# Eight instead of six of 22 pairs of k tiles of each w_down half by seven block products

## The reference

```python
h = rmsnorm(x, g_ffn_pre[l])
ff = (jax.nn.silu(h @ w_gate[l]) * (h @ w_up[l])) @ w_down[l]
x = x + rmsnorm(ff, g_ffn_post[l])
```

## Time and profile before

| | us |
|---|---|
| median of 3 runs | 1199.53 |
| lowest, highest | 1198.66, 1199.59 |
| profiled execution, its own time | 1201.28 |
| its span in the trace | 1199.6 |
| PE busy | 1184.5 |
| DVE busy | 986.0 |
| ACT busy | 686.1 |
| POOL busy | 77.5 |

### The profile page before, as it was taken

One profiled execution on the slowest core, in us unless ns is written; L12 is line 12 of the kernel. 1 busy time (PEld: TensorE's weight loads), 2 busy tenths in 40 slices (PEclk: granted clock), 3 DMA queues, 4 the chain that ended last, 5 costly groups with the idle time before them and its releaser, 6 DMA issues.

```text
span 1199.6 us, 16437 instructions
## 1 busy us (share of the span) xinstructions
PE 1184.5 (99%) x5733; PEld 993.7 (83%) x5733; DVE 986.0 (82%) x1314; ACT 686.1 (57%) x924; POOL 77.5 (6%) x85
## 2 busy tenths in 40 slices
PE   8999999999999999999999999999999999999997
PEld 7888888888888888888888888888888888888885
DVE  6656777876786755879999999999999789879877
ACT  5654666474654744665556566665655555546543
POOL 1000100000000000001110110111010001000100
PEclk9999999999999999999999999999999999999999
DMA  8656867767785655566575667657565766655653
GB/s 313 207 158 158 226 174 157 181 141 183 184 188 173 224 186 195 173 235 195 193 239 185 202 207 228 202 182 247 187 198 200 246 210 211 210 176 196 213 188 140
DMA packets 124596, 237.23 MB, mean 198 GB/s; under 512 B 8312, under 2 KB 24960, under 8 KB 123392
## 3 DMA queue, kind: packets, MB, share of 16 engines
q1 hardware_dynamic: 122784, 231.05, 62.1%
q0 software_dynamic: 1760, 5.51, 1.7%
HBM read 229.97 MB, written 4.20 MB: 195 GB/s over the span
## 4 chain that ended last, share of the span: by engine, by line
PE 87%; DVE 5%; DMA 5%; ACT 1%; issue 1%; SPq 0%; DVEq 0%; ACTq 0%
PE bank L1787 85%; DMA raw<-in_w_in 4%; DVE w_lo L1132 2%; DMA resid<-in_x 1%; PE bank L2064 1%; ACT w_hi L711 1%; DVE w_lo L1618 0%; PE bank L1792 0%; PE bank L1981 0%; DVE more_lo L1618 0%; DVE raw L1635 0%; DVE v_sb L1259 0%; DVE gT L1346 0%; DVE h L1159 0%; DVE resid L1780 0%
## 5 line engine op out<-in xcount | busy, mean ns | idle before, releaser
L1132 DVE TENSOR_TENSOR w_lo<-raw,w_hi 128x1024 fp32r<-128x1024 f32 x172 | 209.2, 1223 | 121.6 <-ACT w_hi L711 121.1
L711 ACT ACTIVATE w_hi<-raw 128x1024 fp32r<-128x1024 f32 x172 | 180.5, 1057 | 164.5 <-PE bank L1787 142.4
L1787 PE MATMUL bank<-hT,w_hi 128*128 128x512 f32 x768 | 270.7, 396 | 1.4 <-DVE w_lo L1132 1.4
L1787 PE MATMUL bank<-w_hi,h2T 128*128 128x512 f32 x778 | 253.4, 391 | 0.0
L1787 PE MATMUL bank<-hT,w_lo 128*128 128x256 f32 x768 | 214.5, 279 | 0.0
L1787 PEld LDWEIGHTS bank<-hT,w_hi 128*128 128x128 f32 x768 | 143.9, 187 | 33.5 <-DVE w_lo L1132 2.0
L1787 PEld LDWEIGHTS bank<-w_hi,h2T 128*128 128x128 f32 x778 | 146.1, 188 | 30.1
L1615 DVE TENSOR_TENSOR w_lo<-raw,w_hi 128x1024 fp32r<-128x1024 f32 x110 | 133.5, 1230 | 19.4 <-ACT w_hi L1022 18.6
L1787 PE MATMUL bank<-w_lo,h2T 128*128 128x512 f32 x379 | 147.5, 389 | 0.0
L1787 PEld LDWEIGHTS bank<-hT,w_lo 128*128 128x128 f32 x768 | 145.0, 189 | 0.0
L1618 DVE TENSOR_TENSOR w_lo<-raw,w_hi 128x1024 fp32r<-128x1024 f32 x126 | 134.6, 1105 | 2.3 <-ACT w_hi L1036 1.7
(11 more groups left out here) (265 smaller groups left out, 1808.4 us busy)
## 6 DMA issues: line engine op xcount, KB each, us to landing
raw<-in_w_in SPq DMA_DIRECT2D x63, 1024.0 KB, 11.0
raw<-in_w_down SPq DMA_DIRECT2D x88, 512.0 KB, 5.0
raw<-in_w_up SPq DMA_DIRECT2D x80, 512.0 KB, 3.9
raw<-in_w_gate SPq DMA_DIRECT2D x80, 512.0 KB, 4.7
raw<-in_w_out SPq DMA_DIRECT2D x16, 1024.0 KB, 5.0
raw<-in_w_gate SPq DMA_DIRECT2D x4, 1024.0 KB, 5.2
raw<-in_w_up SPq DMA_DIRECT2D x4, 1024.0 KB, 6.4
raw<-raw POOLq DMA_DIRECT2D x9, 256.0 KB, 5.7
```

The lines of the kernel that those rows point to most:

```text
L711: act.activation(part_of(w_hi, rnd, s), src, ACT.Copy).then_inc(hi_done, 1)
L1132: dve.tensor_tensor(part_of(w_lo, rnd, s), raw_sub(rnd, s)[1], part_of(w_hi, rnd, s).bitcast(F32), ALU.subtract).then_inc(lo_done, 1)
L1787: return pe.matmul(out_, lhsT, rhs, start=start, stop=stop, skip_group_check=True)
```

## The change

Two plan strings differ. The first half (`DOWN`) had S units 3, 6, 9, 12, 15 and 18, and has 3, 5, 8, 10, 13, 15, 18 and 20. The second half (`LAST_HALF`) had 2, 5, 8, 11, 14 and 17, and has 3, 5, 7, 9, 11, 13, 15 and 17. All counts of pieces, loads, waits and sums follow from the strings. Each half has 60 pieces instead of 56. The last S unit of the first half is unit 20 instead of 18, so that one R unit stands behind it, where there were three.

```diff
 FULL = Plan("RRSSRSSR")
 FINAL = Plan("RRSSRRRR")
-DOWN = Plan("RRRSRRSRRSRRSRRSRRSRRR")
-LAST_HALF = Plan("RRSRRSRRSRRSRRSRRSRRRR")
+DOWN = Plan("RRRSRSRRSRSRRSRSRRSRSR")
+LAST_HALF = Plan("RRRSRSRSRSRSRSRSRSRRRR")
 LAST_HALF.pieces[-8:] = [(n, piece) for piece in range(2) for n in range(18, 22)]
 DOWN_PLANS = (DOWN, LAST_HALF)
```

## The result

The changed kernel takes 1202.98 us (median of 10 runs, 1202.03 to 1204.23) against 1199.56 for the kernel before (10 runs). The ratio is 1.0027, 95% interval 1.0019 to 1.0035: slower by 3.4 us, where 4.8 was forecast. The profiled execution took 1203.55 us.

The account below looks back on a forecast made before the run. PE was taken to bound the kernel while VectorE delivers. Second half: stalls 0.6 + 6.2 + 0.1 = 6.9 us less 1.36 of products, +5.5; first half -0.7; together +4.8 on 1199.53, so 1204.3 us, range 1201.9 to 1206.9.

Parts of the forecast that it names:

- The bound: w_down halves: PE bounds while VectorE delivers; afterwards VectorE bounds the second half's R S stretch; 58% for this forecast.
- The price of a pair: VectorE time per unit: S 8.06 us plus 1.11 for a GpSimd collision, R 2.28; R S 11.45 against PE's 10.21.
- Unit 5 of the second half: Its operands, ready 1.1 us early before the change, come late and stall PE by 0.6 us.
- T: The time at which PE starts the second half, 1075.67 before; VectorE's partial sums were to start at T - 4.5.
- The last period: Second half, unit 15 to 17: no GpSimd subtraction left, VectorE takes 10.34 us, 0.1 us of stall.
- The first half: 0.7 us of stall at unit 5, taken between 0.1 and 1.2, less 1.36 of products: -0.7 us.
- The gap at unit 3: First half's first S unit: PE's wait for operands stays at 0.72 us, as unit 3 is S before and after.
- collisions cost little: Rival for both halves: GpSimd collisions fall where VectorE waits, no stall, net -2.7 us, 1196.8 us; 6%.
- half of them land harmless: Rival: half the collisions are harmless or more lead is handed over; stalls 3 to 4.5 us, 1200.5 us; 9%.
- a second chain joins: Rival, second half: ScalarE's rounding also delays VectorE, 0.4 us in each of six periods, +2.4 us, 1206.7 us; 10%.
- The first half stalled less than forecast and not more: Rival: first half stalls 1.2 us at unit 5 and 0.5 at units 10 and 15, +1.5 us, 1205.8 us; 15%.
- the partial sums were done: Rival at the half boundary: VectorE over 1.9 us behind with the partial sums, so PE stops, +1 us more; 2%.

Follow-up runs that it names:

- experiment 3: Changed kernel with GpSimd subtracting only 8 of the 512 columns for each w_down S unit; 1196.61 us, ratio 0.9964 to the kernel before.
- experiment 6: Changed kernel with GpSimd's subtraction replaced by a ScalarE negation and an adding DMA; 1196.50 us, ratio 0.9967 to the kernel before.
- experiment 7: Changed kernel with GpSimd writing a constant to the same block instead of subtracting; 1196.72 us, ratio 0.9964 to the kernel before.
- experiment 4: Kernel before with seven S units in each half, 3 5 8 10 13 15 18 and 3 5 8 10 13 15 17; 1197.74 us, ratio 0.9980.
- experiment 2: Kernel before with only the second half changed to eight S units, six in the first as before; 1203.22 us, ratio 1.0028.
- experiment 10: Kernel before, old plans, with only the block sum moved from GpSimd to ScalarE and a DMA; 1198.94 us, ratio 0.9993.
- experiment 1: Kernel before with only the first half changed to eight S units, six in the second as before; 1198.26 us, ratio 0.9985.
- experiment 5: Kernel before with eight S units in the first half and seven in the second (3 6 8 11 13 15 17); 1197.46 us, ratio 0.9977.
- experiment 8: Changed kernel with GpSimd doing its subtraction twice for each w_down S unit; 1215.64 us, ratio 1.0125 to the kernel before.

## Why the prediction was right, point by point

- *The bound.* Right. The chain shows PE's unbroken run broken up in the second half and nowhere else, and there PE starts each S unit 0.06 us after L1749. That d_ops is the deadline that ends last, before w_lo, is what PE's timeline shows.
- *The price of a pair.* 8.06 + 2.28 = 10.34 us for R S without a collision: 10.35 in experiments 3, 6 and 7. The collision was priced 1.11 and is 0.97 here. It falls on the d_sum of L1725 and not on L1749. That this d_sum has only 128 columns is not the reason: in experiment 4 the one of L1722 lost the full 1.1 us (at 1145.71, below). L1725 begins 0.32 us behind L1722, where two d_sum without a pause are 0.20 apart; that it so comes 0.12 late to GpSimd's instruction would fit, but was not tested. So a period is 11.32 instead of 11.45. In five periods that is 0.7 of the 6.2 us. It is the largest term that was mis-sized.

```profile
1144.64 2.31 POOL L671 TENSOR_TENSOR raw<-raw 128x512 f32<-128x512 f32 x1 [8.01 <-DMA raw<-in_w_down]
1145.71 1.38 DVE L1722 TENSOR_TENSOR d_sum<-d_sum,d_whole 128x128 f32<-128x128 f32 x1
```

- *Unit 5 of the second half.* The operands were to come 0.6 us late; PE was held up by 0.3. VectorE began its partial sums at T - 4.6 instead of T - 4.5, and the two collisions on the way cost 0.97 each. The delay by the last S unit at 20 was real: experiment 2, without it, has unit 5 early by 1.1.
- *The last period* without a collision: 10.35, so 0.14 of stall, as said. In all 6.0 us of stalls against 6.9; another 0.1 is lost behind unit 17's first product, which no term had.
- *The first half.* 0.7 of stall was taken from between 0.1 and 1.2, and it was 0.3: GpSimd's subtraction for unit 8 came just behind L1749 (it began at 985.85, and L1749 had ended at 985.18). PE lost 0.11 up to unit 5 and 0.17 up to unit 8, 0.09 of that at unit 5's second product. The collision fell on the w_lo of unit 5's fourth piece, which was still ready at 988.56, ahead of the product that reads it (989.03).
- *The gap at unit 3* was to stay at 0.72. It shrank to 0.40. In the kernel before GpSimd's subtraction for unit 6 ran at 970.13, beside the w_lo of unit 3; now the next S unit is 5, its chunk is loaded one unit earlier, and the subtraction ran at 965.04, ahead of that w_lo. No step counted this. The prediction took the three of twelve that didn't cost 1.1 us for harmless; of these only the one beside the partial sums was. The one at 959.26 stood beside a more_lo subtraction of 1024 columns that took 2.08 us instead of 1.21, and this one cost 0.3 us ahead of the gap. The gap is 0.40 in experiments 4 and 6 too, and in experiment 10, which has the old plans without GpSimd's subtraction; in experiment 2, which has them with it, it is 0.77. The w_lo before and after:

```profile
970.13 1.30 POOL L671 TENSOR_TENSOR raw<-raw 128x512 f32<-128x512 f32 x1 [9.56 <-DMA raw<-in_w_down]
971.00 1.51 DVE L1618 TENSOR_TENSOR w_lo<-raw,w_hi 128x1024 fp32r<-128x1024 f32 x1 [1.67 <-ACT w_hi L1036]
...
969.96 1.23 DVE L1618 TENSOR_TENSOR w_lo<-raw,w_hi 128x1024 fp32r<-128x1024 f32 x1 [1.66 <-ACT w_hi L1036]
```

- *The rivals.* That collisions cost little or half of them land harmless, and that a second chain joins, were wrong: the period is VectorE's instructions and the collision in each of the five periods, with nothing in between. The first half stalled less than forecast and not more, and the partial sums were done at 1071.35, 1.8 us before PE began the half at 1073.17.

The mechanism was right. The second half's stalls, the first half's and the gap were off by 0.9, 0.4 and 0.3 us, all on one side, which is why 3.4 was measured for 4.8.

## What to carry to other kernels

When the busiest engine is given less to do by giving a helper more, add up the helper's time over one period of the pattern at the densest place, not over the stage: five units R R S R S fit into PE's time, R S did not, and five periods that were each 1.1 us too long ate twice the 2.7 us that the products of both halves gave back. Put the added work where the helper has slack (experiments 1, 4 and 5 gained with the same trade). And count what a third engine takes from the helper: here the 1.0 us of each GpSimd subtraction was the whole difference between 3.4 us slower and 3 to 4 faster (experiment 6).

## What the runs showed of the hardware

A GpSimd subtraction of 128x512 float32 that reads and writes SBUF held up a VectorE instruction with two SBUF inputs by 0.87 to 1.12 us in the changed kernel's halves, wherever VectorE had no idle time; the seven of L1725 lost 0.97 each, and a d_sum that takes 0.29 alone took 1.26. GpSimd pays too: its subtraction takes 1.30 us alone, 1.54 in the R S period at 1106.40 and 2.39 at 1113.50 in the kernel before. With 8 columns instead of 512 (experiment 3) VectorE's durations grew by no more than 0.01 us, and beside the partial sums, which have one input in PSUM, they kept their 0.69 us. The Trainium skill (SBUF — State Buffer, section "Who interferes with whom") says that such a VectorE instruction contends with a GpSimd one that reads SBUF and not with one that only writes it. Experiment 7 agrees: a GpSimd write of the same block cost VectorE nothing, in any period.

In experiment 8 PE lost 2.2 us in each 12.4, and its granted clock was 0.95 over that stretch, where it is 1.00 in the changed kernel with 1.1 in 11.3:

```profile
1105.26:1167.32 62.06, 55.84 (x226) 44.11 (x226) 61.37 (x71) 31.02 (x36) 17.24 (x10) 0.95 0.51 170
```

The 0.95 is two short falls to 0.50, the level of 1.2 GHz. The first comes behind an idle time of 2.32 us before unit 5; from 1105.9 to 1108.9 the products start 0.43 us apart instead of 0.23:

```profile
1106.39 0.63 PE L1791 MATMUL bank<-w_hi,ffT 128*128 128x512 f32 x1
1106.82 0.63 PE L1791 MATMUL bank<-w_lo,ffT 128*128 128x512 f32 x1
```

The second comes behind an idle time of 1.87 us before unit 11. The idle time of 1.88 us before unit 9 brought none. It cost nothing there, as VectorE set the pace: the two periods with a fall took 12.42 and 12.41 us, and the others 12.41. Whether it would cost time where PE sets the pace was not tried.
